# One more gate in seven block products, with its token sums started behind attention, and the last mLSTM head's division moved ahead of its score weighting

## The reference

```
h = rmsnorm(x, norm1_g)
z = h @ w_in + b_in
mq, mk, mv, mo, mi, mf, fq, fk, fv, ff, gm, gf = split(z)
y_m = mlstm(mq, mk, mv, mi, mf), normalised per head, * sigmoid(mo)     # 4 heads of 128
y_f = forgetting_attention(fq, fk, fv, ff)                              # 8 heads of 64
mix = sigmoid(gm) * (y_m @ w_br_mlstm) + sigmoid(gf) * (y_f @ w_br_fox)
x   = x + mix @ w_out
x   = x + swiglu(rmsnorm(x, norm2_g))
return rmsnorm(x, norm_f_g)
```

## Time and profile before

| | |
|---|---|
| median of 3 runs | 755.36 us (755.12 to 756.07) |
| the profiled execution | 755.58 us, span 753.9 us |
| TensorE busy | 743.4 us, 99% of the span |
| VectorE busy | 565.3 us, 75% |
| ScalarE busy | 326.8 us, 43% |
| mean granted TensorE clock | 0.996 |
| DMA | 75.29 MB, mean 100 GB/s |
| load of one 1 MB slot of w_in, issue to landing | 5.2 us (median of 21) |

### The profile page before, as it was taken

One profiled execution on the slowest core, in us unless ns is written; L12 is line 12 of the kernel. 1 busy time (PEld: TensorE's weight loads), 2 busy tenths in 40 slices (PEclk: granted clock), 3 DMA queues, 4 the chain that ended last, 5 costly groups with the idle time before them and its releaser, 6 DMA issues.

```text
span 753.9 us, 12153 instructions
## 1 busy us (share of the span) xinstructions
PE 743.4 (99%) x4899; PEld 659.9 (88%) x4899; DVE 565.3 (75%) x859; ACT 326.8 (43%) x512; POOL 24.0 (3%) x51
## 2 busy tenths in 40 slices
PE   8999999999999999999999999999999999999996
PEld 7988889988676788998889899999999998888885
DVE  5878899867978588986257899999999998433123
ACT  5553235655555343453235444444444446333211
POOL 4000000011100000000000000000000000000000
PEclk9999999999999999999999999999999999999999
DMA  8533304411111112417412213333333234322202
GB/s 243 151 112 112 98 15 140 131 38 57 57 57 58 57 57 70 155 58 283 134 57 79 90 58 111 113 113 112 112 112 89 89 105 168 112 103 69 108 1 112
DMA packets 61805, 75.29 MB, mean 100 GB/s; under 512 B 3682, under 2 KB 49842, under 8 KB 61748
## 3 DMA queue, kind: packets, MB, share of 16 engines
q1 hardware_dynamic: 61744, 74.50, 30.6%
q10 hardware_dynamic: 4, 0.00, 0.0%
HBM read 72.40 MB, written 2.10 MB: 99 GB/s over the span
## 4 chain that ended last, share of the span: by engine, by line
PE 72%; issue 1%; DVE 0%; ACT 0%; POOLq 0%; POOL 0%; ACTq 0%
PE bank L1635 23%; PE bank L1637 22%; PE bank L1636 22%; PE bank L1933 1%; PE bank L1895 1%; PE bank L1916 1%; PE bank L1902 0%; PE bank L1648 0%; PE bank L1899 0%; DVE w_lo L988 0%; ACT square_out L568 0%; ACT x L950 0%; DVE x L1607 0%; DVE work L1259 0%; POOLq L171 0%
## 5 line engine op out<-in xcount | busy, mean ns | idle before, releaser
L988 DVE TENSOR_TENSOR w_lo<-stage,w_hi 128x1024 fp32r<-128x1024 f32 (+1 forms) x125 | 137.0, 1105 | 95.2 <-ACT w_hi L591 86.3
L1635 PE MATMUL bank<-hT_hi,w_hi 128*128 128x256 f32 (+1 forms) x572 | 182.5, 319 | 0.3 <-DVE hT_lo L973 0.3
L1637 PE MATMUL bank<-hT_hi,w_lo 128*128 128x256 f32 (+1 forms) x572 | 179.9, 314 | 0.0
L1636 PE MATMUL bank<-hT_lo,w_hi 128*128 128x256 f32 (+1 forms) x572 | 179.8, 314 | 0.0
L591 ACT ACTIVATE w_hi<-stage 128x1024 fp32r<-128x1024 f32 x126 | 121.0, 964 | 125.3 <-PE bank L1637 114.5
L1635 PE MATMUL bank<-t_hi,w_hi 128*128 128x256 f32 x432 | 122.3, 283 | 0.0
L1636 PE MATMUL bank<-t_lo,w_hi 128*128 128x256 f32 x432 | 122.3, 283 | 0.0
L1637 PE MATMUL bank<-t_hi,w_lo 128*128 128x256 f32 x432 | 122.3, 283 | 0.0
L1637 PEld LDWEIGHTS bank<-hT_hi,w_lo 128*128 128x128 f32 x572 | 109.0, 191 | 6.8
L1635 PEld LDWEIGHTS bank<-hT_hi,w_hi 128*128 128x128 f32 x572 | 109.1, 191 | 6.7 <-issue 0.4
L1636 PEld LDWEIGHTS bank<-hT_lo,w_hi 128*128 128x128 f32 x572 | 109.2, 191 | 5.8
(11 more groups left out here) (221 smaller groups left out, 1093.8 us busy)
## 6 DMA issues: line engine op xcount, KB each, us to landing
stage<-in_w_in SPq DMA_DIRECT2D x21, 1024.0 KB, 5.2
stage<-in_w_gate SPq DMA_DIRECT2D x11, 1024.0 KB, 5.4
stage<-in_w_up SPq DMA_DIRECT2D x11, 1024.0 KB, 5.4
stage<-in_w_down SPq DMA_DIRECT2D x22, 512.0 KB, 4.5
stage<-in_w_out SPq DMA_DIRECT2D x4, 1024.0 KB, 8.3
x_nat<-in_x SPq DMA_DIRECT2D x4, 512.0 KB, 5.7
stage<-in_w_br_mlstm SPq DMA_DIRECT2D x4, 512.0 KB, 3.5
stage<-in_w_br_fox SPq DMA_DIRECT2D x4, 512.0 KB, 4.5
```

The lines of the kernel that those rows point to most:

```text
L988: dve.tensor_tensor(ring_part(w_lo, g), staged(g), ring_part(w_hi, g).bitcast(F32), ALU.subtract).then_inc(lo_split, 1)
L1635: pe.matmul(o, a_hi, b_hi, start=first, stop=False)
L1636: pe.matmul(o, a_hi, b_lo, start=False, stop=False)
L1637: return pe.matmul(o, a_lo, b_hi, start=False, stop=last)
```

## The change

Three edits. (1) Round 1's gf slot becomes a seven slot; its granules are B0 to B3, and the tanh of gf reads the quarters, as in rounds 2 and 3. (2) The token sums of this stage are moved forward: additions 0 and 1 ahead of the last `take_yfT_lo`, addition 2 behind it, 3 to 5 behind round 0, 6 and 7 inside B's run; the splits into `t_hi` and `t_lo` follow in the order 0, 1, 2, 3, here and in the earlier stage of fq and fk, and TensorE's waits for them are cut in finer steps. (3) `head_output(2)` stands ahead of `weigh_scores(3)`.

```
@@ slots
         (seven_slot if i >= 2 else column_slot)(w_in, C_GM + 2 * P * i)
-        (seven_slot if i >= 2 else column_slot)(w_in, C_GF + 2 * P * i)
+        (seven_slot if i >= 1 else column_slot)(w_in, C_GF + 2 * P * i)
@@ scalar
-                    for n in range(4):
+                    for n in range(2):
                         hi_ahead(g + n)
                         if n == 0:
                             take_mix_hi(1)
+                            take_t_hi(0, 5, 1)
+                            take_t_hi(1, 6, 1)
                         act.wait_ge(used, g + n + 1)
                         act.wait_ge(mix_step, 3 * 2 * c - (1 if n % 2 else 4))
                         gate_tanh_of(c, n, GATE_BANKS[n])
-                        for m, n_steps in BR_T_HI_AT[n]:
-                            take_t_hi(m, n_steps, 1)
-                    g += 4
+                    hi_ahead(g + 2)
+                    take_t_hi(3, 8, 1)
+                    keep_first(g + 2)
+                    for n in range(3, 6):
+                        hi_ahead(g + n)
+                    g += 6
@@ vector
             for h in range(H_M):
                 mask_stabiliser(h)
+                if h == H_M - 1:
+                    head_output(h - 1)
                 weigh_scores(h)
-                if h >= 1:
+                if 1 <= h < H_M - 1:
                     head_output(h - 1)
...
+            token_sums(0, 1)
+            token_sums(1, 1)
             take_yfT_lo(KB - 1)
+            dve.wait_ge(fox_pv, FOX_PAIRS)
+            token_sums(2, 1)
...
                     if c == 1:
-                        for n in range(4):
-                            lo_ahead(g + n)
-                            if n == 0:
-                                take_mix_lo(1)
-                            for step in BR_T_STEPS_AT[n]:
-                                token_sums(step, 1)
-                            for m, count in BR_T_LO_AT[n]:
-                                take_t_lo(m, count, 1)
+                        lo_ahead(g)
+                        take_mix_lo(1)
+                        take_t_lo(0, 2, 1)
+                        take_t_lo(1, 3, 1)
+                        lo_ahead(g + 1)
+                        take_t_lo(2, 1, 1)
+                        g += 2
+                        lo_ahead(g)
+                        token_sums(6, 1)
+                        token_sums(7, 1)
+                        take_t_lo(3, 4, 1)
+                        lo_ahead(g + 1)
+                        run_sums(g, 0)
+                        run_sums(g, 1)
+                        lo_ahead(g + 2)
+                        run_sums(g, 2)
+                        run_sums(g, 3)
+                        run_sums(g, 4)
+                        lo_ahead(g + 3)
...
+                if c == 0:
+                    for step in range(3, 6):
+                        token_sums(step, 1)
@@ tensor, in_seven
-                    pe.wait_ge(t_lo_ready, 4 * side(g) + 3)
+                    pe.wait_ge(t_lo_ready, 4 * side(g) + T_LO_STEPS[side(g)][0])
...
+                if i == 0 or side(g) != side(runs[i - 1]):
+                    pe.wait_ge(t_lo_ready, 4 * side(g) + 3)
@@ tables
-BR_RUNS_AT = ((6, 4, 5, 7), (2, 0, 1, 3))
+BR_RUNS_AT = ((5, 7, 6, 4), (6, 4, 5, 7), (2, 0, 1, 3), (2, 0, 1, 3), (6, 4, 5, 7))
```

More of the change, by code:

```diff
@@ L381, in run_banks @@
             if g < G_FFN:
-                return BR_RUNS_AT[(runs.index(g) - FQ_RUNS + 1) // 2 % 2]
+                return BR_RUNS_AT[runs.index(g) - FQ_RUNS]
             if g in ffn_first:
@@ L818, in gate_tanh_pair @@
             def gate_tanh_pair(c, n):
-                act.wait_ge(up_step, UP_STEPS * (FQ_RUNS + 2 * (c - 2) + n // 2 + 1))
+                act.wait_ge(up_step, UP_STEPS * (FQ_RUNS + 2 * c - 2 + n // 2))
                 for m in range(n, n + 2):
@@ L854, in _ @@
                     hi_ahead(g + j)
-                    if c >= 2 and j == 0:
+                    if c == 0 and j == 0:
+                        take_t_hi(2, 3, 1)
+                    if c >= 1 and j == 0:
                         gate_tanh_pair(c, 2)
@@ L1048, in run_sums @@
                     if G_BR <= g < G_FFN:
-                        dve.wait_ge(gate_tanh, 8 + 2 * (i - FQ_RUNS))
+                        dve.wait_ge(gate_tanh, 6 + 2 * (i - FQ_RUNS))
                     elif g in ffn_first:
@@ L1075, in tile @@
                     return t_sum[s][a][:, :, :] if a in (0, 1, 2) else a[0][:, a[1][0], a[1][1]].bitcast(F32)
-                dve.wait_ge(*((t_step, 8 * s + step) if step else (norm[s // 2]["hT_lo_ready"], 2 * ROWS) if s != 1 else (fox_pv, FOX_PAIRS)))
+                dve.wait_ge(*((t_step, 8 * s + step) if step else (norm[s // 2]["hT_lo_ready"], 2 * ROWS)))
                 if step == 6:
-                    dve.wait_ge(t_lo_ready, 4 * s + 2)
+                    dve.wait_ge(t_lo_ready, 4 * s + T_LO_STEPS[s][1])
                 dve.tensor_tensor(t_sum[s][out][:, :, :], tile(a), tile(b), op).then_inc(t_step, 1)
@@ L1466, in _ @@
                         take_mix_lo(b - 1)
-                    if c == 1 and j == 0:
-                        take_t_lo(3, 4, 1)
                     dve.wait_ge(used, g + j + 1)
@@ L1993, in _ @@
                 if c == 1:
-                    for n in range(4):
+                    for n in range(2):
                         z_columns(g0 + n, GATE_BANKS[n], (gate_tanh, 4 * c + n + 1))
+                    in_seven(g0 + 2)
+                    g0 += 2
                 elif c >= 2:
@@ L2105 @@
 FQ_T_HI_AT = {1: ((2, 3),), 2: ((0, 5), (1, 6))}
[L2106 to L2109, removed]
+FQ_T_LO_AT = {2: ((0, 2), (1, 3), (2, 1))}
 T_HOME = (1, 0, 2, 2)
+T_LO_STEPS = ((2, 3), (2, 3), (3, 2))
 T_STEPS_AT = {(0, 0): (0, 1), (0, 1): (2, 3), (0, 2): (4,), (0, 3): (5,), (1, 0): (6,), (1, 1): (7,)}
```

## The result

The changed kernel takes 757.78 us (median of 7 executions, 756.97 to 758.37), the kernel before 755.32 (7 executions, 755.12 to 756.07). The ratio is 1.0030, with a 95% interval of 1.0021 to 1.0039: slower by about 2.3 us. The predicted 756.8 is 1.0 too low; the range of 755.9 to 758.6 holds the time, the forecast's own 756.1 to 757.4 doesn't. The profiled execution took 757.72 us, with a span of 756.0, 2.1 more than before. Of this, round 1 is +3.72 and the stretch from `mlstm_values(2)` to A0 is -0.96. The start of the kernel (-0.37) and what lies behind D0 (-0.29) are the rest, and no edit explains those two. Both also differ, by 0.25 and 0.16, between the profiles of before and of the head-only kernel, whose code is the same there.

The account below looks back on a forecast made before the run. TensorE, busy 743.4 of 753.9 us, was taken to bound the kernel. Head -0.90, matmuls -0.81, new waits +2.74 and +0.38 sum to +1.41 us on 755.36, so 756.8; range 755.9 to 758.6.

Parts of the forecast that it names:

- the forecast's own 756.1 to 757.4: Whole kernel: the range for the forecast case of 756.8 us, without the rivals; chance 0.45.
- The matmuls: Round 1's gf slot: 84 matmuls of 256 tokens replace 48 of 512, a gain of 0.81 us.
- The head: Last mLSTM head: the earlier division ends TensorE's 0.73 us wait at `mlstm_values(3)`; gain 0.9 us in all.
- should nearly close: Last mLSTM head, line 1933: TensorE's 0.3 us wait nearly goes, since VectorE gains about 1.0 us.
- the bound of 1.03: Last mLSTM head: upper bound on the gain from the earlier division, taken as 0.9 us; lower bound 0.4.
- VectorE's list: Round 1: VectorE's operations laid out from 261.19 give TensorE new waits of 2.74 and about 0.38 us.
- A new wait of 2.74 us: Round 1, last of B's seven products: TensorE wants B3 at 280.50 and gets it at about 283.24.
- The second wait: Round 1, at C0: its low part is ready at 285.00, TensorE at 284.68; a wait of about 0.38 us.
- third wait: Round 2, at D0: forecast none; a rival had a late weight load make D0 1 us late, 757.8, chance 0.05.
- The sum: Whole kernel: -0.90 - 0.81 + 2.74 + 0.38 = +1.41 us on the median of 755.36, giving 756.8.
- the first rival: Round 1: the clock falls in the new wait, +1.0 to +1.4 us more, 757.7 to 758.3; chance 0.37.
- The skill's pace: Round 1's gf slot: N/2.4 + 2.5 ns per isolated matmul would give 1.19 us; the prediction used its rows instead.

Follow-up runs that it names:

- head-only kernel: Edit 3 (`head_output(2)` ahead of `weigh_scores(3)`) alone on the kernel before; 754.56 us, ratio 0.9986.
- sums in gaps: Changed kernel with B3's and C0's splits moved forward on ScalarE and VectorE, plus token addition 3 and `t_lo` 2 in VectorE's earlier idle time; 753.68 us, ratio 0.9976.
- The three experiments that shorten the chain step by step: Changed kernel with B3's and C0's splits earlier on ScalarE, then also on VectorE, then also two VectorE operations in earlier idle time; 755.74, 754.94, 753.68 us.
- matmuls in the wait: Changed kernel with 21 additional matmuls of 256 tokens, results overwritten, in TensorE's wait ahead of B3; 757.05 us, ratio 1.0018.
- gate-only kernel: Changed kernel with edit 3 taken back, so edits 1 and 2 alone on the kernel before; 759.31 us, ratio 1.0047.
- the two kernels with splits first: Changed kernel with B3's and C0's splits moved forward, on ScalarE only (755.74 us, ratio 1.0003) or on VectorE as well (754.94 us, ratio 0.9992).

## Why the prediction had the waits right and the clock wrong

**The matmuls, right.** The prediction has 0.81 us for 84 halved against 48 whole ones; where no wait follows, round 1 is shorter by 0.78, and B alone by 0.81 (10.07 us, from 270.90 to 280.97 with sums in gaps).

**The head, right, with parts of another size.** Predicted 0.9; 1.1 by the times. In the traces it is 0.89 at `mlstm_values(3)` (4.97 us against 5.86), where I had 0.73: the idle time that a row shows counts from the modelled end of the last matmul, not from when the next could have begun. The wait at the first product with the values, which "should nearly close", stayed at 0.3. That product, and the operation of VectorE that it waits for, before and after:

```profile
198.96 0.68 DVE L1259 TENSOR_TENSOR work<-bank,o_gate 128x512 f32<-128x512 f32 x1
199.79 0.44 PE L1933 MATMUL bank<-pT,v_f 128*64 128x128 f32 x4 [0.30 <-DVE work L1259]
...
197.58 0.68 DVE L1266 TENSOR_TENSOR work<-bank,o_gate 128x512 f32<-128x512 f32 x1
198.41 0.44 PE L1960 MATMUL bank<-pT,v_f 128*64 128x128 f32 x4 [0.31 <-DVE work L1266]
```

Counted from `mlstm_values(2)` (180.17 before, 179.80 after), both come 1.01 us sooner. VectorE gained the 1.0 that the prediction gave it; since TensorE gained as much, the wait between them stayed. So the gain up to here is 1.01, just inside the bound of 1.03.

**VectorE's list, right.** "A new wait of 2.74 us" shows as 2.69, ended by the `w_lo` that the prediction named; in the prediction's own count, from when TensorE could have begun, it is 2.85. From A0 to the restart it said 283.24 - 260.99 = 22.25 us, and it is 282.02 - 259.66 = 22.36. The copy into `parts` starts 0.11 after `t_lo` 3 ends (279.00 + 1.23 against 280.34), not within 0.1 but near it. The second wait, "about 0.38", comes to 0.36 where the clock stays up, 0.1 of it the slow first step, and is hidden where the clock falls, since TensorE then comes to C0 later than C0 is ready. No third wait appeared. The three experiments that shorten the chain step by step bring the wait from 2.69 to 1.54, to 1.04 and to none, and the time falls with each.

**The clock, the step that failed.** The sum left the clock where it was, a term of nothing, and made its fall the first rival, at 0.37 against 0.45. It came out the other way: the clock fell in the profiled execution, at 1.18 us of round 1, inside the rival's +1.0 to +1.4. The measured 757.78 lies in the rival's 757.7 to 758.3; the range held it because it was drawn to reach over that rival. With matmuls in the wait the kernel takes 757.05, 1.41 more than before on that chip, and the sum said +1.41. That it fits to the hundredth is luck: the head gave some 0.1 to 0.2 more than summed, and round 1, at 35.22 us, is 2.58 longer than before where the sum had 2.31. What the prediction should have seen is that its own row had a fall after 1.79 us of idleness while the forecast had TensorE idle for 2.74, and that nothing in the trace spoke for dense work as a protection; the 0.73 us that brought no fall are far shorter than both. It is not certain either: the same wait left the clock up in one profile. From the times, two of the changed kernel's seven executions (756.97 and 757.04) and one of the gate-only kernel's five look like that, but only one of these three was seen in a trace, and the two are only 0.7 to 0.8 below their kernel's profiled execution, less than 1.18. Why the same wait lets the clock fall in one execution and not in another stays open.

**The skill's pace.** By the gap that the Trainium skill (TensorE: Matmul & The Clock Gate, Back-to-back issue gap) gives for isolated matmuls the slot would have given 1.19 us as an estimate; the trace disagrees, with 0.78.

## What to carry to other kernels

Before you move a consumer to an earlier place, follow the last operand that it needs back over every engine, and ask at each step what stands in front of that operation in its engine's list, not only what it depends on. Here B3's split needed nothing of the token sums and still came after all of them, since a copy with a long wait stood ahead of it. Putting the two splits first and moving two operations into gaps turned the whole change's loss of 2.3 us into a gain of 1.9, of which 1.1 is the head's. A wait of TensorE like this one, of 2.7 us, is not priced by its length alone: add what the clock takes if it falls, here 1.18.

## What the runs showed of the hardware

The lower clock costs the two sizes differently. In the changed kernel's profile the matmuls of 512 tokens come 0.427 us apart (three steps from 284.20 to 285.48) where it is 0.2267 at the upper level, a factor of 1.9, and those of 256 tokens 0.212 (five steps from 282.92 to 283.98) against 0.1199, 1.8. And the first matmul after a wait is dearer: 0.22 us to the next (282.02 to 282.24), 0.1 more than in the stream.

The length of an idle stretch doesn't decide alone whether the clock falls. At the start of the kernel, after little work, it was at the lower level behind 1.79 us in the profile of before and behind 1.44 in that of sums in gaps (its wait, and its window of TensorE at the start):

```profile
PE bank L1694 <- DVE xn L1006: 1.4, 1, 1.4
...
8.00:9.00 1.00, 1.00 (x6) 0.50 1.21 324
```

Between the dense matmuls of round 1 it stayed up behind 1.04 and 1.54 us in the profiles of the two kernels with splits first, and behind 2.69 it fell in one profile and stayed up in another. These are single profiles, so they give no threshold.
